# K pages turned on VectorE in 32x32 blocks, and a sample's past split into four partial softmaxes

## The chip, the cores and the metric

The kernel runs on one core of one Trainium2 chip. The metric is the device time of one execution in microseconds (us), lower is better. Three runs of the kernel before gave 971.84, 969.80 and 974.57 us, so the median is 971.84.

## What is computed

One inference step of a two-layer decoder trunk, all in float32, `D_MODEL` 1024, 16 heads of 64. Inputs are a prompt of 512 tokens and 8 sample sequences of 8 new tokens each, whose past of 2048 tokens lies in pages: 16 pages of 128 rows a sample, found through a page table. Layer A is a gated short convolution. Its result gives shared keys, values and log-forget values; layer B is attention over them. The part around the change, cut from the reference:

```python
def _fox_attend(q, fq, qpos, k, v, fk, kpos):
    s = jnp.einsum('nqhd,nkhd->nhqk', q, k).astype(jnp.float32) * (HEAD_DIM ** -0.5)
    s = s + (jnp.transpose(fq, (0, 2, 1))[:, :, :, None]
             - jnp.transpose(fk, (0, 2, 1))[:, :, None, :])
    mask = kpos[None, :] <= qpos[:, None]
    s = jnp.where(mask[None, None], s, -jnp.inf)
    p = jax.nn.softmax(s, axis=-1)
    return jnp.einsum('nqhk,nkhd->nqhd', p.astype(v.dtype), v)

k_past = cache_k[page_table].reshape(nb, -1, N_HEADS, HEAD_DIM)
v_past = cache_v[page_table].reshape(nb, -1, N_HEADS, HEAD_DIM)
```

A sample's attention runs over its 2048 past rows and its 8 new ones; the prompt's over its own 512 rows with a causal mask.

## The kernel before, in words

All is one program of five instruction streams (SP, POOL, ACT, DVE, PE) that wait on semaphores; the order within each is written out by hand. It has four parts: layer A (`mixer`, eight rounds), the output of A in slabs (`out_slab`), eight query blocks (`query`), and then a loop over i = 0..7 (`heads`), followed by a tail that joins the new tokens and makes the output of B.

Round i of the loop does two things at once. It projects K, V and the gate for head pair i, with weights split into a high and a low part (`piece`, L1221; `project(0)`, `(1)`, `(2)`), and does the prompt's attention of that pair in four blocks (`block_scores`, `block_turn`, `block_out`). And it does the past attention of sample i over 32 pages: 16 of K, then 16 of V, each 128 rows by 1024 floats (512 KB).

The pages arrive in a ring of 8 slots in SBUF (`ring`, 4 KB a slot and partition). SP issues all loads of pages, weights, suffix rows and f rows in one order; page n + 8 is loaded when slot n is free (L370 to L377, L431 to L436): for K when the page has been turned (`b_t1`), for V when the product has used it (`b_used`, L434).

In the K stretch, for each page k, PE turns the page in eight 128x128 transposes through two PSUM banks (`turn`, L1201, called under `for k in range(NPG)`); ACT (L666) and DVE (L1009) copy one bank each into `KTS`. After every two pages `unit_scores` (L1404) makes the scores of one unit of 256 rows: the 32 output rows of column group j hold four heads by eight queries, and the query operand `QC` is zero outside of its own heads. DVE adds the forget suffix and takes the maximum (`add_suffix`, L1014). Pieces of `project(0)` and `project(1)` stand between the pages. POOL scales the weights (L501) and copies the next `QC` and `QT`.

Then a bridge: the maximum of the sample, four exponentials on ACT (L707), each of which lets PE turn one group of four 128-column blocks of scores; ACT and DVE copy them to `PTS`. In between stand the turns of the new K and V rows, pieces of `project(2)` and the prompt's block scores.

In the V stretch, for each page k, PE makes four products of 32 by 256 (L1519), accumulated over all 16 pages into bank `OS`:

```python
for j in range(4):
    mm = pe.matmul(PS[32 * j:32 * j + 32, OS, 0:4 * HD], PTS[:, k, 32 * j:32 * j + 32],
                   ring[:, n % RING, 4 * HD * j:4 * HD * (j + 1)],
                   start=(k == 0), stop=(k == NPG - 1), tile_position=(0, 32 * j))
```

Only one quarter of the columns of each 256-wide product belongs to each output row's head. The prompt's steps stand between the pages. At the end ACT copies the result to `OPAST`, and DVE (L1123, L1127) gates and splits the prompt's output of the pair.

In the tail PE makes the new tokens' scores (L1537), DVE and ACT their softmax joined with the past, PE the products (L1565), DVE the merge (L1167, L1169), PE turns it back, while tiles of the output projection (`early_tile`, L1270) fill the gaps.

A float32 matmul leaves two records in the trace, a transpose and a split (float32r) matmul one.

## Time and profile before

| | |
|---|---|
| runs | 971.84, 969.80, 974.57 us |
| profiled execution | 975.04 us, of which the span is 973.2 us |
| granted TensorE clock | 0.996 of full speed |
| loop over the samples | 364 to 899 us |
| instructions in the span | 23705 |
| DMA over the span | 212 GB/s mean; the K and V page loads are 256 of 512 KB |

The page gives each engine's busy share and the span in 40 slices; a view of windows gives the same for any stretch, with the share of time that the 16 DMA engines had packets in flight. TensorE overlaps its matmuls, so the mean of one record is longer than its share of the busy time: costs are taken as busy time divided by count.

### The profile page before, as it was taken

To read this page: it belongs to the slowest core of one execution; us is meant where nothing else is said; L and a number is where in the kernel's file an instruction comes from. 1 tells how busy PE (TensorE), PEld (TensorE's weight loads), DVE (VectorE), ACT (ScalarE), POOL (GpSimd) and SP (SyncE) were. 2 spreads that over 40 slices of the span, in tenths; PEclk is the share of its full clock that TensorE was granted. 3 is DMA by queue.
4 is the path that set the end of the run, shared out by engine and by line. 5 is a ranking of instruction groups with operands and counts; after the bars stand their busy time and mean duration, and the time that the engine had idled before them with its cause. 6 is when DMAs were issued, how large, how long until landed. Compare 5 with 4: busy or idle time off the path is not lost.

```text
span 973.2 us, 23705 instructions
## 1 busy us (share of the span) xinstructions
PE 939.5 (97%) x8516; PEld 802.0 (82%) x8516; DVE 486.6 (50%) x1133; ACT 385.1 (40%) x728; POOL 167.4 (17%) x111
## 2 busy tenths in 40 slices
PE   4999999999999999999999999999999999999998
PEld 4999999999998987868768778688687686776898
DVE  5675444556355334554544544645545545445632
ACT  5333333332144443543444534535434445345210
POOL 2233444332030311102002002011020020000000
PEclk9999999999999999999999999999999999999999
DMA  7233222225343527799799798798996997987412
GB/s 233 66 87 86 86 76 75 85 65 130 120 165 103 174 55 228 254 329 341 237 360 313 249 364 290 247 376 261 315 350 237 362 323 244 365 297 249 142 44 98
DMA packets 133334, 206.41 MB, mean 212 GB/s; under 512 B 8848, under 2 KB 91457, under 8 KB 133171
## 3 DMA queue, kind: packets, MB, share of 16 engines
q1 hardware_dynamic: 121602, 198.35, 60.7%
q10 hardware_dynamic: 11168, 5.51, 2.0%
q0 software_dynamic: 528, 2.10, 0.8%
q8 instruction: 21, 0.34, 0.2%
q14 instruction: 15, 0.11, 0.0%
HBM read 195.29 MB, written 10.63 MB: 212 GB/s over the span
## 4 chain that ended last, share of the span: by engine, by line
PE 82%; DMA 7%; ACT 4%; DVE 4%; issue 2%; SPq 1%; ACTq 0%; DVEq 0%
PE psum L1221 40%; PE psum L1201 16%; PE psum L1270 9%; PE psum L1404 7%; PE psum L1519 4%; DMA page_ring<-in_cache_k 4%; ACT sample_scores L707 2%; DMA w_raw<-in_a_w_out 2%; PE psum L1469 1%; PE psum L1447 1%; DMA residual<-in_x_prompt 1%; PE psum L1319 1%; PE psum L1427 1%; PE psum L1449 1%; DMA page_ring<-in_cache_v 1%
## 5 line engine op out<-in xcount | busy, mean ns | idle before, releaser
L1221 PE MATMUL psum<-xn_high,w_high 128*128 128x256 f32 (+1 forms) x992 | 237.2, 318 | 2.6 <-DVE w_low L832 2.6
L1221 PE MATMUL psum<-xn_low,w_high 128*128 128x256 f32 (+1 forms) x992 | 216.4, 297 | 0.0
L1221 PE MATMUL psum<-xn_high,w_low 128*128 128x256 f32 (+1 forms) x992 | 216.3, 297 | 0.0
L1221 PEld LDWEIGHTS psum<-xn_high,w_high 128*128 128x128 f32 x992 | 163.9, 191 | 20.2 <-issue 16.6
L1221 PEld LDWEIGHTS psum<-xn_high,w_low 128*128 128x128 f32 x992 | 169.0, 191 | 0.0
L1221 PEld LDWEIGHTS psum<-xn_low,w_high 128*128 128x128 f32 x992 | 168.9, 190 | 0.0
L1201 PE MATMUL psum<-constants,page_ring 128*128 128x128 f32 x1024 | 137.5, 277 | 7.7 <-DMA page_ring<-in_cache_k 6.5
L1201 PEld LDWEIGHTS psum<-constants,page_ring 128*128 128x128 f32 x1024 | 114.8, 141 | 35.1 <-issue 33.4
L501 POOL TENSOR_TENSOR w_raw<-w_raw,gains 128x1024 f32<-128x1024 f32 x32 | 60.8, 1899 | 338.9 <-DMA w_raw<-in_b_w_in 220.7
L1009 DVE COPY k_turned_odd<-psum 128x512 f32<-128x512 f32 x64 | 44.2, 691 | 93.5 <-PE psum L1201 93.5
L832 DVE TENSOR_TENSOR w_low<-w_raw,w_high 128x1024 fp32r<-128x1024 f32 x32 | 51.4, 1606 | 72.6 <-ACT w_high L565 72.6
L1009 DVE COPY k_turned<-psum 128x512 f32<-128x512 f32 x64 | 44.2, 690 | 71.5 <-PE psum L1201 71.3
L478 POOL TENSOR_TENSOR w_raw<-w_raw,gains 128x1024 f32<-128x1024 f32 x30 | 62.5, 2083 | 88.7 <-DMA w_raw<-in_a_w_in 88.7
L666 ACT ACTIVATE k_turned<-psum 128x512 f32<-128x512 f32 x64 | 38.2, 597 | 96.5 <-PE psum L1201 96.4
L1519 PE MATMUL psum<-page_ring,p_turned 128*32 128x256 f32 x1024 | 75.2, 388 | 0.9 <-DMA page_ring<-in_cache_v 0.8
L565 ACT ACTIVATE w_high<-w_raw 128x1024 fp32r<-128x1024 f32 x32 | 33.9, 1060 | 89.0 <-PE psum L1221 63.5
L666 ACT ACTIVATE k_turned_odd<-psum 128x512 f32<-128x512 f32 x64 | 38.1, 596 | 71.3 <-PE psum L1201 71.3
L1270 PE MATMUL psum<-w_high,gated_high 128*128 128x256 f32 (+1 forms) x160 | 46.5, 290 | 4.4 <-DVE w_low L859 1.9
L926 DVE TENSOR_TENSOR w_low<-w_raw,w_high 128x1024 fp32r<-128x1024 f32 x30 | 36.9, 1231 | 18.2 <-ACT w_high L615 18.2
L1270 PE MATMUL psum<-w_low,gated_high 128*128 128x256 f32 (+1 forms) x160 | 45.7, 286 | 0.0
L1270 PE MATMUL psum<-w_high,gated_low 128*128 128x256 f32 (+1 forms) x160 | 45.7, 286 | 0.0
L1270 PE MATMUL psum<-w_high_b,gated_high 128*128 128x256 f32 (+1 forms) x160 | 45.3, 283 | 0.1
(236 smaller groups left out, 1420.2 us busy)
## 6 DMA issues: line engine op xcount, KB each, us to landing
page_ring<-in_cache_k SPq DMA_DIRECT2D x128, 512.0 KB, 5.6
page_ring<-in_cache_v SPq DMA_DIRECT2D x128, 512.0 KB, 4.8
w_raw<-in_a_w_in SPq DMA_DIRECT2D x30, 512.0 KB, 4.1
suffix<-suffix_scratch SPq DMA_DIRECT2D x32, 256.0 KB, 4.8
w_raw<-in_b_w_in SPq DMA_DIRECT2D x16, 512.0 KB, 6.2
w_raw<-in_kv_w SPq DMA_DIRECT2D x16, 512.0 KB, 6.1
w_raw<-in_a_w_out SPq DMA_DIRECT2D x4, 1024.0 KB, 5.1
f_broad<-f_scratch SPq DMA_DIRECT2D x8, 512.0 KB, 6.2
```

The source lines that it names most:

```text
L478: pool.tensor_tensor(WR[:, q % 2, :, :], WR[:, q % 2, :, :], gain(G_A), ALU.mult).then_inc(a_scaled, 1)
L501: pool.tensor_tensor(WR[:, slot, :, :], WR[:, slot, :, :], gain(g), ALU.mult).then_inc(b_scaled, 1)
L565: act.activation(WH[:, slot, :, :], WR[:, slot, :, :], ACT.Copy).then_inc(a_high, 1)
L666: return act.activation(out, src, ACT.Copy)
L832: dve.tensor_tensor(WL[:, slot, :, :], WR[:, slot, :, :], WH[:, slot, :, :].bitcast(F32), ALU.subtract).then_inc(a_split, 1)
L926: dve.tensor_tensor(lo, WR[:, slot, :, :], h.bitcast(F32), ALU.subtract).then_inc(b_split, 1)
L1009: return dve.tensor_copy(out, src)
L1201: return pe.transpose(out, src, CT[0:r, C_ID:C_ID + r])
L1221: mm = pe.matmul(PS[:, bank + h, 0:c.stop - c.start], w[:, k, :], x[:, k, c], start=(k == 0 and n == 0), stop=(k == KT - 1 and n == 2))
L1270: mm = pe.matmul(PS[0:r, bank, 0:SLAB], x[:, k, toks(t)], wp[:, k, :], start=(k == 0 and p == 0), stop=(k == KT - 1 and p == 2))
L1404: mm = pe.matmul(PS[32 * j:32 * j + 32, bank, 0:256], QC[:, 2 * j + pp, :], KTS[u % 2][:, 2 * j + pp, :], start=(pp == 0), stop=(pp == 1), ...
L1519: mm = pe.matmul(PS[32 * j:32 * j + 32, OS, 0:4 * HD], PTS[:, k, 32 * j:32 * j + 32], ring[:, n % RING, 4 * HD * j:4 * HD * (j + 1)], star ...
```

## The change

Instead of a whole turn on PE, DVE turns each K page in place in its ring slot, each 32x32 block by itself. After that partition 32a + c of block column m holds, for the rows of quarter a (32 rows), dimension 32m + c. So each quarter of the 128 partitions has its own 32 rows of the page, and 32 of a head's 64 dimensions. The queries are laid out to fit: `QN` holds them with every 32 dimensions repeated on all four quarters, and `QC` is made by POOL for each sample (`spread_queries`), with eight query columns for each quarter and zeros outside of the own one. A score row is now (group of heads j, quarter r, query), its columns (head x in the group, row in the quarter); a head's two halves of dimensions are accumulated (f = 0, 1). Each row's maximum and sum are over one head and a quarter of all past rows: four partial softmaxes for each query, whose maxima (`MS`) and sums (`LS`) have four columns a sample. They are joined once, in the tail.

V goes with it. `vpages` orders a page's rows as (r p): one transfer puts row 32r + p on partition a + 4p, slot r of half a ring; four pages fill every partition of four slots. So V is used by groups of four pages, `b_v` counts whole groups, and SP waits for four V steps before it refills (n = 16 and 20). The turned probabilities (`PTS`) are multiplied by POOL onto the diagonal blocks of a zeroed tile, `PTZ` (one buffer, four times a sample, waiting for the V steps of the group before), so that a product has the rows of its quarter alone.

A K slot is free only when its unit is scored (`b_su`). The scores are 32 matmuls a unit with 64 columns, V 16 a page with 64 columns; all keep 128 rows by 32 columns of weights. The adds of the suffix go by group of four pages and head: four of 128 columns in place of two of 256. The suffix rows are stored in the new order (`SP`). `SS` exponentials are one for each head x over all groups, and PE waits for all four.

Ahead of the loop PE makes `QN` by 16 matmuls of 512 columns with slices of the identity, copied by ACT and DVE; `KTS`, `QZ`, `CK` and `CQ` go. Constants are shorter. In the tail the maxima are turned, joined over the quarters, turned back; the new tokens' scores are 128 matmuls of 8 columns; sums are joined by a matmul with `SUM`; DVE scales `OPAST` by sample (8 multiplies), and 16 matmuls with a summing operand merge the quarters on top of the new tokens' products, so that the result is already turned.

The diff's core (the rest is semaphore counts, placements and the tail):

```diff
@@ -373,10 +396,15 @@
 
         def load_page(b, n):
             page = sp.value_load(PTAB[0:1, bass.ds(b * NPG + n % NPG, 1)], min_val=0, max_val=n_pool - 1)
-            src = (kpages if n < NPG else vpages)[bass.ds(page, 1), :, :]
-            sp.dma_start(ring[:, n % RING, :], src.rearrange("a p n -> (a p) n")).then_inc(b_page[n % RING], 16)
-
-        sp.wait_ge(s_table, 16 * 3)
+            if n < NPG:
+                src = kpages[bass.ds(page, 1), :, :].rearrange("a p n -> (a p) n")
+                sp.dma_start(ring[:, n % RING, :], src).then_inc(b_page[n % RING], 16)
+            else:
+                half, a = n // GROUP % 2, n % GROUP
+                src = vpages[bass.ds(page, 1), :, :, :].rearrange("a p r n -> (a p) r n")
+                sp.dma_start(ring[a:P:GROUP, GROUP * half:GROUP * half + GROUP, :], src).then_inc(b_v[half], 16)
...
                         sp.wait_ge(b_used, NPG * i + n - NPG + 1)
                         sp.dma_start(X[0:rows(t), t, :], h_dram[t * P:t * P + rows(t), :]).then_inc(s_hld, 16)
                 else:
-                    sp.wait_ge(s_table, 16 * 3)
-                    if n < NPG:
-                        sp.wait_ge(b_t1, 24 * i + n + 1)
-                    else:
+                    sp.wait_ge(s_table, 16 * 4)
+                    if n < RING:
+                        sp.wait_ge(b_su, NPG // 2 * i + n // 2 + 1)
+                    elif n < NPG and n % GROUP == 0:
+                        sp.wait_ge(b_su, NPG // 2 * i + (n + GROUP) // 2)
+                    elif NPG <= n < NPG + RING and n % GROUP == 0:
+                        sp.wait_ge(b_used, NPG * i + n - NPG + GROUP)
+                    elif n >= NPG + RING:
                         sp.wait_ge(b_used, NPG * i + n - NPG + 1)
                     load_page(i + (n + RING) // STREAM, (n + RING) % STREAM)
...
+        def spread_queries(b):
+
+            q = QN[:, :, bass.ds(b * NQ, NQ)].unsqueeze(2).to_broadcast([P, 2 * H, GROUP, NQ])
+            own = QM[:, :].unsqueeze(1).unsqueeze(3).to_broadcast([P, 2 * H, GROUP, NQ])
+            pool.tensor_tensor(QC[:, :, :].rearrange("p c (r q) -> p c r q", r=GROUP), q, own, ALU.mult).then_inc(b_qc, 1)
+
...
+        ones = CT[:, T_ONE:T_ONE + 1].unsqueeze(2).unsqueeze(3).to_broadcast([P, GROUP, 4 * XQ, NQ])
 
         def heads(i, last):
...
+            for g in range(NG):
+                pool.wait_ge(b_used, NPG * i + GROUP * g)
+                pool.wait_ge((b_t0f, b_t1f)[g % 2], 8 * i + 3 + g // 2)
+                blocks = PTS[:, GROUP * g:GROUP * g + GROUP, :].rearrange("p x (j r q) -> p r (x j) q", j=XQ, r=GROUP)
+                pool.tensor_tensor(diagonal, blocks, ones, ALU.mult).then_inc(b_pz, 1)
+            if last:
...
-                                     bias=TINY[:, 13:14], accum_out=TINY[:, 16 + c:17 + c])
-                ins.then_inc(b_es, 1)
+            for x in range(XQ):
+                s4 = SS[:, :].rearrange("p (g x n) -> p x g n", g=NG, x=XQ)[:, x]
+                act.activation(s4, s4, ACT.Exp, bias=TB[:, x:x + 1], accum_out=TL[:, x:x + 1]).then_inc(b_es, 1)
...
@@ -1004,52 +1055,48 @@
...
+            def add_suffix(g):
+
+                free, bank = ((b_c0f, C0), (b_c1f, C1))[g % 2]
+                dve.wait_ge(b_sfx[g % 2], (2 * i + g // 2 + 1) * 16)
+                dve.wait_ge(b_su, NPG // 2 * i + 2 * g + 2)
+                dve.memset(TINY[0:1, 32 + g:33 + g], 0.0)
+                for x in range(XQ):
+                    out = SS[:, (XQ * g + x) * P:(XQ * g + x + 1) * P].rearrange("p (n a) -> p a n", a=GROUP)
+                    scored, later = (z.rearrange("p (a x n) -> p x a n", a=GROUP, x=XQ)[:, x]
+                                     for z in (PS[:, bank, :], SFX[:, g % 2, :]))
+                    ins = dve.tensor_tensor_reduce(out, scored, later, 1.0, NEG, ALU.add, ALU.max, TM[:, x, g:g + 1])
+                ins.then_inc(free, 1)
 
             for k in range(NPG):
-                c = (k % 2) * PAGE
-                if k % 2 and k >= 3:
-                    u = k // 2 - 1
-                    if u % 2 == 0:
-                        dve.wait_ge(b_sfx[(u // 2) % 2], (2 * i + u // 4 + 1) * 16)
-                    dve.wait_ge((b_c0, b_c1)[u % 2], 8 * i + u // 2 + 1)
+                dve.wait_ge(b_page[k % RING], (2 * i + k // RING + 1) * 16)
+                dve.transpose(ring[:, k % RING, :], ring[:, k % RING, :]).then_inc(b_kt, 1)
+                if k % GROUP == 1 and k >= GROUP:
+                    add_suffix(k // GROUP - 1)
                 if k == 6:
...
-                turned1(KTS[k // 2 % 2][:, 4:8, c:c + PAGE],
-                        PS[:, T1, :].rearrange("p (k n) -> p k n", k=4)).then_inc(b_t1f, 1)
-                if k % 2 and k >= 3:
-                    add_suffix(k // 2 - 1)
                 if k == 11:
...
@@ -1360,17 +1421,24 @@
         pe.wait_ge(q_rr, KT - 1)
         q_sum()
         pe.wait_ge(s_fnr, 1)
-
+        pe.wait_ge(q_out, KT)
+        pe.wait_ge(s_bf, 6)
+        for c in range(4):
+            for r in range(XQ):
+                mm = pe.matmul(PS[32 * r:32 * r + 32, T0 + c, :].rearrange("p (m n) -> p m n", m=KT),
+                               CT[:, C_ID + 32 * c:C_ID + 32 * c + 32], QF[:, :, SEQ:TOK],
+                               start=True, stop=True, tile_position=(0, 32 * r))
+        mm.then_inc(s_qs, 1)
 
         def heads(i):
             t0, t1 = [0], [0]
...
             def unit_scores(u):
 
-                full, free, bank = ((b_c0, b_c0f, C0), (b_c1, b_c1f, C1))[u % 2]
+                free, bank = ((b_c0f, C0), (b_c1f, C1))[u // 2 % 2]
                 if u == 0:
                     pe.wait_ge(b_qc, i + 1)
-                    pe.wait_ge(q_out, KT)
-                pe.wait_ge(free, 8 * i + u // 2)
-                pe.wait_ge(b_t0f, 24 * i + 2 * u + 2)
-                pe.wait_ge(b_t1f, 24 * i + 2 * u + 2)
-                for pp in range(2):
-                    for j in range(4):
-                        mm = pe.matmul(PS[32 * j:32 * j + 32, bank, 0:256], QC[:, 2 * j + pp, :],
-                                       KTS[u % 2][:, 2 * j + pp, :],
-                                       start=(pp == 0), stop=(pp == 1), tile_position=(0, 32 * j))
-                mm.then_inc(full, 1)
+                    pe.wait_ge(s_qn, 4)
+                if u % 2 == 0:
+                    pe.wait_ge(free, 6 * i + u // 4)
+                pe.wait_ge(b_kt, NPG * i + 2 * u + 2)
+                slot = 2 * u % RING
+                for x in range(XQ):
+                    for f in range(2):
+                        for j in range(QH):
+                            c = 2 * (QH * j + x) + f
+                            out = PS[32 * j:32 * j + 32, bank, 256 * (u % 2):256 * (u % 2) + 256]
+                            mm = pe.matmul(out.rearrange("p (a x n) -> p x a n", a=2, x=XQ)[:, x], QC[:, c, :],
+                                           ring[:, slot:slot + 2, 32 * c:32 * c + 32],
+                                           start=(f == 0), stop=(f == 1), tile_position=(0, 32 * j))
+                mm.then_inc(b_su, 1)
...
-                page = ring[:, k % RING, :]
-                free0()
-                for p in range(4):
-                    mm = turn(PS[:, T0, p * P:(p + 1) * P], page[:, p * P:(p + 1) * P])
-                mm.then_inc(b_t0, 1)
-                free1()
-                for p in range(4):
-                    mm = turn(PS[:, T1, p * P:(p + 1) * P], page[:, (4 + p) * P:(5 + p) * P])
-                mm.then_inc(b_t1, 1)
                 if k == 9:
 
...
             project(2, [3])
 
             for g in range(4):
-                pe.wait_ge(b_es, 4 * i + g + 1)
+                if g == 0:
+                    pe.wait_ge(b_es, 4 * i + 4)
...
-                n = NPG + k
-                pe.wait_ge(b_page[n % RING], (4 * i + n // RING + 1) * 16)
+                g, r = k // GROUP, k % GROUP
                 if k == 0:
                     pe.wait_ge(b_ln, i + 1)
-                if k % 4 == 0:
-                    g = k // 4
-
-                    pe.wait_ge((b_t0f, b_t1f)[g % 2], 24 * i + 19 + g // 2)
-                for j in range(4):
-                    mm = pe.matmul(PS[32 * j:32 * j + 32, OS, 0:4 * HD], PTS[:, k, 32 * j:32 * j + 32],
-                                   ring[:, n % RING, 4 * HD * j:4 * HD * (j + 1)],
-                                   start=(k == 0), stop=(k == NPG - 1), tile_position=(0, 32 * j))
+                    pe.wait_ge(b_sot, i)
+                if r == 0:
+                    pe.wait_ge(b_v[g % 2], 16 * GROUP * (2 * i + g // 2 + 1))
+                    pe.wait_ge(b_pz, NG * i + g + 1)
+                for x in range(XQ):
+                    for j in range(QH):
+                        h = QH * j + x
+                        c = 4 * P * r + P * x + 32 * j
+                        mm = pe.matmul(PS[32 * j:32 * j + 32, OS, x * HD:(x + 1) * HD], PTZ[:, c:c + 32],
+                                       ring[:, GROUP * (g % 2) + r, h * HD:(h + 1) * HD],
+                                       start=(k == 0 and x == 0), stop=(k == NPG - 1 and x == XQ - 1),
+                                       skip_group_check=True, tile_position=(0, 32 * j))
                 mm.then_inc(b_used, 1)
-            assert t0[0] == t1[0] == 24
+            assert t0[0] == t1[0] == 8
 
         with pe.Fori(0, NB) as i:
             heads(i)
 
 
```

The tail's merge (added lines):

```diff
+        pe.wait_ge(m_pd, XQ)
+        for m in range(KT):
+            for e in range(2):
+                h = 2 * m + e
+                pe.matmul(PS[64 * e:64 * e + 64, C0, m * NS:(m + 1) * NS], VS[:, h * HD:(h + 1) * HD],
+                          PD[:, h, :, :].rearrange("p b q -> p (b q)"),
+                          start=(m == 0), stop=False, skip_group_check=True, tile_position=(0, 64 * e))
+        pe.wait_ge(m_w, NB)
+        first = SUM[:, :].rearrange("p (j r q) -> p j r q", j=XQ, r=GROUP)[:, :, 0, :]
+        merged = PS[:, C0, :].rearrange("p (j y b q) -> p y b j q", j=XQ, y=2, b=NB)
         for b in range(NB):
...
-                mm.then_inc(m_pv, 1)
-        for n in (3, 4, 5):
+            for y in range(2):
```

## Rows read from the trace of the kernel before

**Rows 1.** The page, busy us (share of the span) and instructions.
```profile
PE 939.5 (97%) x8516; PEld 802.0 (82%) x8516; DVE 486.6 (50%) x1133; ACT 385.1 (40%) x728; POOL 167.4 (17%) x111
```

**Rows 2.** Windows, one sample: us, busy by engine (records), clock, DMA share, GB/s.
```profile
633.60:700.30 66.70, 65.42 (x655) 49.58 (x655) 33.40 (x97) 30.55 (x66) 8.14 (x6) 1.00 0.92 309
```

**Rows 3.** Timeline, the loop's first and last TensorE pieces: start us, us, what.
```profile
364.09 1.04 PE L1201 MATMUL psum<-constants,page_ring 128*128 128x128 f32 x8
...
898.16 0.64 PE L1519 MATMUL psum<-page_ring,p_turned 128*32 128x256 f32 x8 [0.18 <-DMA page_ring<-in_cache_v]
```

**Rows 4.** Windows, stretches of sample 566 to 633.6 us, same columns.
```profile
566.00:606.00 40.00, 39.92 (x367) 33.47 (x368) 16.05 (x37) 14.34 (x25) 7.54 (x5) 0.96 0.92 317
606.00:614.20 8.20, 8.13 (x67) 6.90 (x65) 5.20 (x16) 5.09 (x12) 0.00 (x0) 1.00 0.55 202
614.20:633.60 19.40, 18.63 (x225) 10.65 (x223) 11.79 (x43) 10.38 (x27) 0.62 (x1) 1.00 0.90 289
```

**Rows 5.** Groups by line and shape, TensorE: busy us, mean ns | idle.
```profile
L1201 PE MATMUL psum<-constants,page_ring 128*128 128x128 f32 x1024 | 137.5, 277 | 7.7 <-DMA page_ring<-in_cache_k 6.5 <-DVE k_turned L1009 1.2
L1519 PE MATMUL psum<-page_ring,p_turned 128*32 128x256 f32 x1024 | 75.2, 388 | 0.9 <-DMA page_ring<-in_cache_v 0.8
...
L1404 PE MATMUL psum<-k_turned_odd,q_current 128*32 128x256 f32 x512 | 34.3, 385 | 0.8 <-DVE k_turned_odd L1009 0.2
...
L1537 PE MATMUL psum<-ks_t,q_spread 128*32 128x64 f32 x128 | 2.0, 220 | 0.2 <-issue 0.2
```

**Rows 6.** Groups by line and shape, VectorE, whole run.
```profile
L832 DVE TENSOR_TENSOR w_low<-w_raw,w_high 128x1024 fp32r<-128x1024 f32 x32 | 51.4, 1606 | 72.6 <-ACT w_high L565 72.6
...
L1009 DVE COPY k_turned<-psum 128x512 f32<-128x512 f32 x64 | 44.2, 690 | 71.5 <-PE psum L1201 71.3 <-DVE f_query L997 0.2
L926 DVE TENSOR_TENSOR w_low<-w_raw,w_high 128x1024 fp32r<-128x1024 f32 x30 | 36.9, 1231 | 18.2 <-ACT w_high L615 18.2
```

**Rows 7.** Groups by line and shape, VectorE, 633.6 to 700.3 us.
```profile
L1087 DVE TENSOR_SCALAR probs<-probs,tiny 128x512 f32<-128x512 f32 x2 | 0.9, 484 | 0.0
...
L1073 DVE CUSTOM_DVE_ANT_0 probs_odd<-psum,f_broad 128x128 f32<-128x128 f32 x2 | 0.5, 288 | 0.0
```

**Rows 8.** Timeline, where one sample ends and the next begins.
```profile
632.26 0.64 PE L1519 MATMUL psum<-page_ring,p_turned 128*32 128x256 f32 x8
...
634.53 0.69 DVE L1127 TENSOR_TENSOR gated_low<-squares,gated_high 128x512 f32 x1 [0.93 <-ACT gated_high L766]
```

**Rows 9.** Groups by line and shape, POOL.
```profile
L501 POOL TENSOR_TENSOR w_raw<-w_raw,gains 128x1024 f32<-128x1024 f32 x32 | 60.8, 1899 | 338.9 <-DMA w_raw<-in_b_w_in 220.7 <-DMA w_raw<-in_kv_w 118.2
```

**Rows 10.** Timeline, the first exponential of a sample's scores.
```profile
608.68 0.71 ACT L707 ACTIVATE sample_scores<-sample_scores,tiny 128x512 f32<-128x512 f32 x1
```

**Rows 11.** Timeline, last V product of groups 0, 1 and 2 of four.
```profile
618.94 0.64 PE L1519 MATMUL psum<-page_ring,p_turned 128*32 128x256 f32 x8
...
624.62 0.64 PE L1519 MATMUL psum<-page_ring,p_turned 128*32 128x256 f32 x8
...
628.22 1.07 PE L1519 MATMUL psum<-page_ring,p_turned 128*32 128x256 f32 x16
```

**Rows 12.** Timeline of SP's queue, four V pages issued.
```profile
601.67 4.10 SPq L377 DMA_DIRECT2D page_ring<-in_cache_v  x4
```

**Rows 13.** DMA queues (packets, MB, share), issues (us to landing), 432 to 830 us.
```profile
q1 hardware_dynamic: 51189, 118.58, 86.5%
q10 hardware_dynamic: 6816, 3.34, 3.0%
...
page_ring<-in_cache_v SPq DMA_DIRECT2D x96, 512.0 KB, 4.7
page_ring<-in_cache_k SPq DMA_DIRECT2D x94, 512.0 KB, 5.8
```

**Rows 14.** DMA queues in the first sample, 364 to 432 us.
```profile
q8 instruction: 6, 0.10, 0.6%
```

**Rows 15.** Timeline, the last query is written.
```profile
366.61 0.57 DVE L978 SCALAR_TENSOR_TENSOR q_spread<-psum,gain_q,rsqrt 64x64 f32<-64x64 f32 x2
```

426 lines of the change are left out of this document (231 added, 195 removed).

## The prediction

> **What bounds the kernel now.** I read the page first: TensorE is busy for 939.5 of 973.2 us [rows 1]. Then one sample: from 633.6 to 700.3 us TensorE worked 65.4 of 66.7 us, VectorE 33.4, ScalarE 30.6, and the DMA share was 0.92 [rows 2]. So two resources are near their ends, and taking work from TensorE helps only until the pages' transfers pace the sample. The loop over the samples runs from 364.1 to 898.8 us [rows 3], eight times 66.8. Three stretches cut one sample [rows 4]: K pages (40 us, TensorE busy throughout, VectorE 16.0), a bridge of 8.2 us, the V stretch (19.4 us). In the V stretch the share is 0.90 and in the bridge only 0.55: the ring is full and waits for the first V step.
>
> **The turns.** 1024 K turns are 137.5 us [rows 5], 134 ns each, 17.2 us a sample. TensorE's K stretch falls from 40 to about 23 us, the sample's TensorE work from 66 to 49.
>
> **Scores and V products.** A product of 256 columns becomes four of 64, 32 output rows each; the columns stay the same. A record of 256 columns takes 67 ns in the scores (34.3 us by 512) and 73 in V; the one row with 64 columns and the same 128x32 weights has 128 records in 2.0 us, 15.6 ns each, a quarter [rows 5]. So I take no change. There are 1024 such records a sample in place of 256. Bounds: below, nothing gained, since the columns stay; above, half as much again for each in a long stream (second rival).
> Ahead of all rows stands a rule: the Trainium skill, "TensorE: Matmul & The Clock Gate", section "Wait — 56ns, not 53.3ns?", says that matmuls never start closer than about 25 ns however few columns they have. The 15.6 ns of [rows 5] are against it, in a burst of 128 records; no row shows 1024 a sample.
>
> **VectorE.** Removed in the K stretch: 16 copies of 0.69 us [rows 6] and eight suffix adds of 256 columns. Added: 16 block turns of 128x1024 in SBUF. No row has one. Nearest is the subtraction of L926, 128x1024, 1.23 us [rows 6]. Below: a TENSOR_SCALAR of 512 at 0.48 us [rows 7] makes 0.8 us for 1024. Above: 1.61 us, the same subtraction in the mixers (L832, [rows 6]). I take 1.23. The suffix adds become 4 of 128 columns for each group of four pages; a 128-column one is 0.29 us [rows 7], with hand-over 0.34, so 1.4 us a group. I count from E, the end of the last V product of the sample before (632.9, [rows 8]). VectorE then still has its last subtraction (L1127, to 635.2 or E+2.3, [rows 8]); then 16 turns (19.7), three groups (4.1), one low_b (1.2) and, estimated from the same rows by columns, KN_T and KS (1.2): last page turned at E+28.5, last scores at E+29.5. TensorE could be there at E+23: **VectorE paces the K stretch**, 29.5 us in place of 40. ScalarE loses 16 copies and is on no path. POOL adds a query spread of 1024 elements (1.9 us by its row of that size, [rows 9]) after the last scores, needed 25 us later.
>
> **Bridge.** The chain behind the last scores is four adds (1.4), the shifts (0.5), and now all four exponentials before the first turn of scores (4 x 0.71, [rows 10]; before, the first was enough), a turn (0.5), a copy (0.6), and the new POOL product of 512 elements (half of 1.9, say 1.1), with hand-overs about 8 us. TensorE's own work in the bridge is 8.1 us [rows 4], most of it ahead of these turns. I take 9 us, against 8.2.
>
> **V stretch.** The groups of four V steps took 5.3, 5.7, 4.1 and 3.6 us (from 614.2 to the ends at 619.5, 625.2, 629.3, 632.9, [rows 4, 8, 11]). V now comes in whole groups, since each transfer writes all four slots on every fourth partition. SP used to refill after each V step; now it waits for four, and K pages of the next sample are queued behind that wait. SP issues four pages in 4.1 us [rows 12] and a V page lands 4.7 us after its issue [rows 13], so a group lands 3.1 + 4.7 = 7.8 us after its first issue. Group 2, asked for at 5.3+0.1, lands at 13.2; TensorE arrives at 11.0 and **waits 2.2 us**. Group 3, asked for at 11.1, lands at 18.9; TensorE arrives at 17.3 and waits 1.6. The POOL product between groups (1.1) lies beside a project and block scores, longer than it (groups 1, 2), and beside transfers (group 3). The stretch is 18.7 + 3.8 = 22.5 us. That each V transfer writes 32 partitions costs nothing by my sum: size and row length (4 KB) are as before. Bounds: nothing, and a doubled transfer, the fourth rival.
> **DMA.** A sample moves its 20 MB in 0.9 x 66.8 = 60 us of busy share, part of it packets in flight beside others: 118.58 MB took 86.5% of 398 us [rows 13], while the first V pages came at 1.03 us by their issue [rows 12]. I estimate 32 pages at 1.3 us, and some 13 us for weights, suffixes, f rows and stores: 55 us. With the K-page requests spread over 29 us this keeps up. K page 0 is asked for after V step 9 as before and is there by E.
> A sample is 29.5 + 9 + 22.5 = **61 us** against 66.8: 8 x 5.8 = 46 us gained.
>
> **Instruction stream.** A sample has 655 TensorE records and as many weight loads [rows 2]. In its first pass 6 instruction packets of 16 KB come in (0.10 MB, [rows 14]), in the passes from 432 to 830 us none: only q1 and q10 stand there [rows 13]. The body was kept. It becomes 655 - 128 + 768 = 1295 of each, some 190 KB. No row says whether that is kept. If not, each of 7 jumps back waits for a transfer: between nothing and the 5.8 us of a loaded K page [rows 13]. I take the middle, 2.9. TensorE has some 1.5 us to spare ahead of the second score unit, on which VectorE waits in order; 1.3 us count, **9 us** in all.
> The Trainium skill, "Runtime: NRT & Kernel Launch", section "Instruction fetch mechanics", gives TensorE's store as 128 KiB and says that a taken branch to a page no longer held stalls; the trace agrees as far as the old body goes. By that page the new body is not kept.
>
> **Ahead and behind.** The first sample started at 364.1, under the last query. Now the quartered queries need all queries (written by 367.2, [rows 15]): 32 records of 512 columns (4.2 us at twice 67 ns), copies (1.4), spreading (1.9) beside the first project. Start at 371.3: **+7 us**. The suffix and mask edits move the same elements: 0. In the tail 64 records of 256 columns and 16 + 8 turns go; 256 tiny records, 32 with full weights (134 ns each) and a chain between VectorE and TensorE come, behind eight multiplies of some 0.4: **+2 us**, between -3 and +8.
>
> **Sum.** -46 + 9 + 7 + 2 = -28 us. The profiled execution took 975.0 us (span 973.2), 3.2 above the median of 971.84. From the median: **943 us**.
>
> **Rivals.**
> 1. *Cheap block turns.* At 0.8 us VectorE needs 7 us less, TensorE (23 and its hand-overs) paces the K stretch and a sample is some 57 us: 943 - 32 = 911; with the body kept 902. For it: the 512 columns in SBUF (0.48) beside those from PSUM (0.69), [rows 6, 7]. Against: a turn is no plain copy. 0.18.
> 2. *Small records cost more in a long stream.* At half as much again, 23.4 ns, 1024 cost 8 us more: 4 in the scores (TensorE at 29 with its hand-overs, beside VectorE's 29.5: some 0.7 late) and 1.0 a V group, of which 3 us stay behind the waits. A sample is 64.7 us: 943 + 8 x 3.7 = 973. For it: one burst is all that speaks against. Against: the 15.6 ns is in proportion to the columns. 0.15 (0.04 faster, 0.06 same, 0.05 slower). By the 25 ns of the Trainium skill's "TensorE: Matmul & The Clock Gate" the same sum gives an estimate of 980.
> 3. *Slower, by VectorE.* Each 0.1 us on a block turn makes a sample 1.6 us longer, as the K stretch waits for 16 in turn: from 1.45 us on the gain is gone. At 1.61 us: 943 + 8 x 6.1 = 992. At two passes (2.3 us) 1080. For it: VectorE has no such operation here and the mixers' row is above that point. Against: L926, the row of this loop, is at 1.2. 0.12.
> 4. *The spread V transfer is slow.* If 16 V pages took double, DMA would need 55 + 21 = 76 us a sample: 1060. Only in favour: no row has the pattern. 0.04.
> 5. *The stall between samples or the groups' wait is worse*, 3 to 4 us each sample: about 970. 0.04, same. That the change fails to remove the turns can't be.
> My forecast has 0.47.
>
> **Numbers.** Faster by over 0.5% (what a measurement here can tell, 4.9 us): 0.47 + 0.18 + 0.04 = 0.69. Same: 0.06 + 0.04 = 0.10. Slower: 0.05 + 0.12 + 0.04 = 0.21. The range leaves out the ends of rivals 1, 3 and 4: 905 to 984. The forecast's own range is 925 to 962.
>
> **What would show it.** Right: a sample near 61 us; the block turn at 1.2 us; TensorE idle in the K stretch waiting for VectorE, and before the third and fourth V group for the V transfer; 64-column records at 16 ns each; instruction packets in every sample. Wrong: turns far from 1.2 us, records above 20 ns, TensorE waiting on K pages (then DMA paces), or a V page landing after more than 6 us.

## The result, and the profile after

The changed kernel takes **1080.3 us** (median of 4 runs, 1079.52 to 1082.57) beside 970.82 us for the kernel before on the same chip: a ratio of 1.114, 95% interval 1.108 to 1.120, so 11% slower where 3% faster was forecast. The profiled execution took 1082.57 us, its span 1080.8. Ratios and intervals leave out an execution clearly slower than the others of its kernel, which touches two runs below: one of 1032.22 us in experiment 1 and one of 1011.44 in experiment 3.

The page of the changed kernel first: busy time by engine, the granted clock by slices (in tenths), the packets of instructions.

```profile
PE 912.4 (84%) x13780; PEld 824.3 (76%) x13780; DVE 570.8 (53%) x1268; ACT 308.6 (29%) x586; POOL 219.1 (20%) x151
PEclk9999999999999999698698799898798797796789
q8 instruction: 111, 1.82, 0.8%
```

TensorE is busy for less time than before (912 against 939 us, [rows 1]) in a span that is 108 us longer. Its clock, full nearly everywhere before, dips once or twice in every sample from the second on. Instruction packets went from 21 to 111. VectorE is at 53%: no engine is full any more.

The last product with the gate of each sample (L1170, L1123 before) comes at 443.1 us in the first sample and at 997.9 in the last: 79.3 us a sample, where it was 66.7 ((898.0 - 431.4) / 7). Of the 107.6 us of longer span, 88 are those seven periods, 12 lie up to the end of the first sample, 8 behind the last. One sample in three windows, K stretch, bridge and V stretch (columns: us, busy time of TensorE, weight loads, VectorE, ScalarE, GpSimd, then granted clock, DMA share, GB/s):

```profile
601.50:638.40 36.90, 29.18 (x650) 26.05 (x650) 24.78 (x49) 5.80 (x11) 6.16 (x3) 0.81 0.73 235
638.40:651.50 13.10, 8.92 (x70) 7.59 (x70) 7.24 (x26) 5.60 (x13) 4.75 (x3) 1.00 1.02 318
651.50:681.10 29.60, 22.15 (x606) 17.71 (x606) 12.12 (x42) 9.64 (x26) 3.67 (x4) 0.88 0.76 257
```

Predicted were 29.5, 9 and 22.5 us; each came out 4 to 7 us longer. In the first and the last window the clock is 0.81 and 0.88, TensorE is busy for 29.18 of 36.90 and 22.15 of 29.60 us, and the DMA share is about 0.75: neither TensorE nor the transfers are full there. What TensorE waited for, in the whole run (columns: us in total, times, longest):

```profile
PE psum L1282 <- issue: 44.0, 14, 5.6
PE psum L1584 <- issue: 30.7, 21, 2.3
PE psum L1584 <- DMA page_ring<-in_cache_v: 25.0, 14, 3.7
PE psum L1282 <- ACT squares L738: 15.1, 8, 2.1
PE psum L1584 <- POOL p_spread L574: 5.7, 6, 1.8
PE psum L1476 <- DVE page_ring L1077: 5.1, 7, 2.0
```

The greatest item, 75 us of "issue" ahead of projections (L1282) and V products (L1584), is time in which TensorE waited for nothing that the profile shows. The wait for VectorE's turns, which was to pace the K stretch, is only 5.1 us. A wait that the sum had at nothing is the fourth line, 1.9 us a sample: projections stand behind a squaring on ScalarE (L738), which waits for VectorE to read the same bank (L1085), and VectorE does that in order, behind seven turns and the first suffix adds. Where the 44 us stand is seen at the jump from one sample to the next, TensorE first and VectorE behind it (start, duration, operation, in brackets the idle time before it):

```profile
601.41 0.65 PE L1584 MATMUL psum<-page_ring,p_spread 128*32 128x64 f32 x32
607.62 0.82 PE L1282 MATMUL psum<-xn_high,w_high 128*128 128x256 f32 x2 [5.56 <-issue]
608.24 0.68 PE L1282 MATMUL psum<-xn_low,w_high 128*128 128x256 f32 x2
608.72 0.68 PE L1282 MATMUL psum<-xn_high,w_low 128*128 128x256 f32 x2
...
612.94 0.43 PE L1282 MATMUL psum<-xn_high,w_low 128*128 128x256 f32 x2
613.20 0.43 PE L1282 MATMUL psum<-xn_high,w_high 128*128 128x256 f32 x2
```

```profile
603.89 6.87 DVE L1077 STREAM_TRANSPOSE page_ring<-page_ring 128x1024 f32<-128x1024 f32 x6
618.11 0.38 DVE L1072 CUSTOM_DVE_ANT_1 sample_scores<-psum,suffix 128x128 f32<-128x128 f32 x1 [7.34 <-issue]
```

The last V product ends at 602.1, the first projection starts at 607.6. For the next 5 us the pairs start 0.48 us apart, from 613 on 0.27: the granted clock is 0.51 from 607.7 to 612.9 us and 1.00 from 613 to 618.9, so after the idle time TensorE runs at the lower of its two levels. The seven idle times like this one are 4.5 to 5.6 us long. So the first scores are late, and VectorE, which has turned six pages by 610.8, stands idle for 7.3 us in front of the suffix add of the first group, with ten more turns in order behind it. The queue of instruction packets in the seven later samples, 443 to 997 us (packets, MB, share):

```profile
q8 instruction: 84, 1.38, 1.1%
```

That is 12 packets of 16 KB a sample, where the kernel before fetched none after its first pass [rows 13, 14].

The operations that the prediction priced without a row (columns: count, busy us, mean ns, then idle time):

```profile
L1077 DVE STREAM_TRANSPOSE page_ring<-page_ring 128x1024 f32<-128x1024 f32 x128 | 150.3, 1217 | 1.0 <-DMA page_ring<-in_cache_k 1.0
L1476 PE MATMUL psum<-page_ring,q_current 128*32 128x64 f32 x4096 | 77.0, 230 | 7.6 <-DVE page_ring L1077 5.1 <-issue 2.4
```

The block turn took 1.22 us (1.23 was taken). At the full clock a unit of scores is 64 records in 1.03 us, 16.1 ns each, and a V step 32 records in 0.57 us, 17.9 ns; no change of the cost by column, 16.8 and 18.3 ns, was taken. Over the whole run, with the stretches at the lower clock, they are 18.8 ns (77.0 us by 4096) and 25.5 ns (L1584, 104.5 us by 4096).

The bridge: GpSimd's queue in front of the first V product.

```profile
646.72 1.90 POOL L537 TENSOR_TENSOR w_raw<-w_raw,gains 128x1024 f32<-128x1024 f32 x1 [13.95 <-DMA w_raw<-in_kv_w]
648.58 1.90 POOL L548 TENSOR_TENSOR q_current<-q_quarters,own_quarter 128x1024 f32<-128x1024 f32 x1
650.43 1.04 POOL L574 TENSOR_TENSOR p_spread<-p_turned,constants 128x512 f32<-128x512 f32 x1
```

A weight scaling, waiting for its transfer, and the query spread for the next sample are ahead of the product that TensorE needs. Then the V stretch: the third group, and gaps of the stream inside it.

```profile
662.01 0.89 PE L1584 MATMUL psum<-page_ring,p_spread 128*32 128x64 f32 x32
668.00 1.94 PE L1584 MATMUL psum<-page_ring,p_spread 128*32 128x64 f32 x64 [3.66 <-DMA page_ring<-in_cache_v]
670.90 0.63 PE L1584 MATMUL psum<-page_ring,p_spread 128*32 128x64 f32 x26
673.29 0.76 PE L1584 MATMUL psum<-page_ring,p_spread 128*32 128x64 f32 x38 [1.76 <-issue]
675.33 1.08 PE L1584 MATMUL psum<-page_ring,p_spread 128*32 128x64 f32 x32 [0.43 <-POOL p_spread L574]
```

```profile
657.77 10.64 SPq L405 DMA_DIRECT2D page_ring<-in_cache_v  x8
```

The third group is asked for at 657.8 and its products start at 668.0; two V steps then take 1.94 us in place of 1.1, at a granted clock of 0.50. The gap ahead of 673.3 splits a V step behind its 26th record, where no wait stands in the code.

Last, the tail: from the end of the loop's last sample to the end, 8 us more than before. Its largest new piece:

```profile
1022.99 7.03 PE L1653 MATMUL psum<-sum_quarters,o_past 128*128 128x32 f32 x32
```

The granted clock is 0.50 through these records.

### The profile page after: what moved, and what is told of

Same layout as the page of the kernel before. It is cut to its first block, busy times and chain, and to the rows that moved or that the text cites. A ratio compares the mean times of both kernels' runs of the same rounds, so it can differ in the third digit from the quotient of the medians.

```text
span 1080.8 us, 33756 instructions
## 1 busy us (share of the span) xinstructions
PE 912.4 (84%) x13780; PEld 824.3 (76%) x13780; DVE 570.8 (53%) x1268; ACT 308.6 (29%) x586; POOL 219.1 (20%) x151
## 4 chain that ended last, share of the span: by engine, by line
PE 57%; issue 18%; DVE 11%; DMA 6%; ACT 3%; SPq 3%; POOL 1%; DVEq 0%; ACTq 0%; POOLq 0%
PE psum L1282 31%; PE psum L1331 8%; PE psum L1584 6%; DVE page_ring L1077 5%; PE psum L1262 4%; DMA page_ring<-in_cache_v 4%; PE psum L1476 3%; SPq L405 1%; SPq L398 1%; ACT sample_scores L762 1%; PE psum L1531 1%; DMA page_ring<-in_cache_k 1%; DMA w_raw<-in_a_w_out 1%; PE psum L1509 1%; DVE sample_scores L1072 1%
## 5 line engine op out<-in xcount | busy, mean ns | idle before, releaser
L1282 PE MATMUL psum<-xn_high,w_high 128*128 128x256 f32 (+1 forms) x992 | 242.0, 324 | 62.2 <-issue 44.0
L1282 PEld LDWEIGHTS psum<-xn_high,w_high 128*128 128x128 f32 x992 | 173.3, 200 | 79.7 <-issue 54.3
L1282 PE MATMUL psum<-xn_low,w_high 128*128 128x256 f32 (+1 forms) x992 | 224.2, 306 | 0.0
L1282 PE MATMUL psum<-xn_high,w_low 128*128 128x256 f32 (+1 forms) x992 | 223.8, 306 | 0.0
L1282 PEld LDWEIGHTS psum<-xn_high,w_low 128*128 128x128 f32 x992 | 176.9, 199 | 0.0
L1282 PEld LDWEIGHTS psum<-xn_low,w_high 128*128 128x128 f32 x992 | 176.8, 199 | 0.0
L1584 PE MATMUL psum<-page_ring,p_spread 128*32 128x64 f32 x4096 | 104.5, 256 | 61.4 <-issue 30.7
L1077 DVE STREAM_TRANSPOSE page_ring<-page_ring 128x1024 f32<-128x1024 f32 x128 | 150.3, 1217 | 1.0 <-DMA page_ring<-in_cache_k 1.0
L1584 PEld LDWEIGHTS psum<-page_ring,p_spread 128*32 128x32 f32 x4096 | 82.4, 131 | 86.9 <-issue 73.6
L1476 PE MATMUL psum<-page_ring,q_current 128*32 128x64 f32 x4096 | 77.0, 230 | 7.6 <-DVE page_ring L1077 5.1
L1476 PEld LDWEIGHTS psum<-page_ring,q_current 128*32 128x32 f32 x4096 | 65.2, 116 | 20.5 <-issue 12.7
L1060 DVE COPY probs_t<-psum 128x512 f32<-128x512 f32 (+3 forms) x32 | 15.7, 491 | 112.7 <-PE psum L1262 112.7
L574 POOL TENSOR_TENSOR p_spread<-p_turned,constants 128x512 f32<-128x512 f32 x32 | 33.4, 1044 | 182.8 <-PE psum L1584 166.2
L1072 DVE CUSTOM_DVE_ANT_1 sample_scores<-psum,suffix 128x128 f32<-128x128 f32 x128 | 35.0, 384 | 58.9 <-issue 58.9
L981 DVE TENSOR_TENSOR w_low<-w_raw,w_high 128x1024 fp32r<-128x1024 f32 x30 | 42.8, 1425 | 25.5 <-ACT w_high L676 25.5
L976 DVE TENSOR_TENSOR residual<-psum,residual 128x256 f32<-128x256 f32 (+1 forms) x40 | 16.7, 421 | 72.2 <-PE psum L1331 72.1
```

The lines of the kernel that those rows point to most:

```text
L981: dve.tensor_tensor(lo, WR[:, slot, :, :], h.bitcast(F32), ALU.subtract).then_inc(b_split, 1)
L1072: ins = dve.tensor_tensor_reduce(out, scored, later, 1.0, NEG, ALU.add, ALU.max, TM[:, x, g:g + 1])
L1077: dve.transpose(ring[:, k % RING, :], ring[:, k % RING, :]).then_inc(b_kt, 1)
L1282: mm = pe.matmul(PS[:, bank + h, 0:c.stop - c.start], w[:, k, :], x[:, k, c], start=(k == 0 and n == 0), stop=(k == KT - 1 and n == 2))
L1476: mm = pe.matmul(out.rearrange("p (a x n) -> p x a n", a=2, x=XQ)[:, x], QC[:, c, :], ring[:, slot:slot + 2, 32 * c:32 * c + 32], start=(f ...
L1584: mm = pe.matmul(PS[32 * j:32 * j + 32, OS, x * HD:(x + 1) * HD], PTZ[:, c:c + 32], ring[:, GROUP * (g % 2) + r, h * HD:(h + 1) * HD], sta ...
```

## Experiments

The theory after the result (A): TensorE's loop body, the instructions of one sample with some 1294 records, is no longer kept from one pass to the next, so each jump back to its start stalls TensorE for 5.5 to 7 us, and slow clock and a late VectorE follow. Rivals: TensorE would have to wait there anyway (B), every packet stalls (C), small records are dear (D).

**1. Jump removed.** In the changed kernel, and as a control in the one before, TensorE's eight samples are written out one behind the other:

```diff
-        with pe.Fori(0, NB) as i:
-            heads(i)
+        for i in range(NB):
+            heads(i)
```

> The kernel after, with TensorE's eight samples written out one behind the other, so that TensorE never jumps back. Theory A (the loop body of 1295 TensorE records a sample is too large to be kept, each jump back stalls TensorE for 5.5 to 7 us, the stall lowers the granted clock for some 5 us and makes VectorE's first suffix add late): the 5 to 7 us of idle time ahead of each sample's first record go, a sample falls from 79.3 to 68 to 71 us, the total from 1080 to 990 to 1015. Instruction packets stay near 100. Rival B (TensorE would have to wait there anyway, for VectorE's turns, the page transfers or the small records' issue): the idle time moves to another releaser and the total stays above 1055. Rival C (it isn't the jump but every instruction packet that stalls TensorE): the idle time is spread over the sample as stalls of 1 to 2 us and the total stays within 20 us of 1080.

Measured: 1025.65 us (1016.15 to 1032.22), ratio to before 1.053 [1.046, 1.060]; a sample takes 71.0 us ((934.0 - 437.2) / 7), 8.3 less. B and C as stated are out: the idle time at the jump is gone, and only a part came back as waits for V and GpSimd. It is A, though the total lies above its 990 to 1015. The gaps ahead of V products fell too, from 30.7 to 4.9 us, so most of them came with the loop; those ahead of scores rose from 2.4 to 10.3. What TensorE now waited for:

```profile
PE psum L1584 <- DMA page_ring<-in_cache_v: 38.8, 16, 4.1
PE psum L1584 <- POOL p_spread L574: 13.2, 6, 3.2
PE psum L1476 <- issue: 10.3, 9, 2.7
PE psum L1584 <- issue: 4.9, 5, 2.3
```

The three stretches of one sample, without the jump (columns as above):

```profile
652.90:682.70 29.80, 26.19 (x621) 23.37 (x620) 25.08 (x48) 5.81 (x11) 5.17 (x3) 0.94 0.89 302
682.70:694.80 12.10, 8.89 (x72) 7.55 (x73) 8.38 (x30) 6.69 (x16) 4.75 (x3) 1.00 0.97 326
694.80:724.70 29.90, 23.34 (x607) 18.75 (x607) 11.35 (x38) 8.55 (x23) 3.81 (x4) 0.80 0.76 266
```

Over the last seven samples the K stretch takes 29.6 to 31.6 us, the bridge 10.1 to 13.4, the V stretch 27.0 to 29.9. So the K stretch is at its forecast of 29.5 once the jump is gone, and the V stretch is not.

> The kernel before, with TensorE's eight samples written out. Its loop body fetches nothing after the first pass, so this prices straight fetching by itself: about 45 more instruction packets. Theory A: hidden, within 5 us of the kernel before (971). Rival C (every packet stalls TensorE by 1 to 2 us): 40 to 80 us more, near 1030.

Measured: 974.44 us, ratio 1.0042 [1.0022, 1.0062], a sample 66.6 us, 36 packets in seven samples. 36 x 16 KB / (7 x 655) is 128 bytes for a record and its weight load. Straight fetching of the old body costs 0.4%.

**2. The body alone made larger.** The kernel before, with V products cut (here all 16 steps):

```diff
-                for j in range(4):
-                    mm = pe.matmul(PS[32 * j:32 * j + 32, OS, 0:4 * HD], PTS[:, k, 32 * j:32 * j + 32],
-                                   ring[:, n % RING, 4 * HD * j:4 * HD * (j + 1)],
+                for x in range(4):
+                    for j in range(4):
+                        c = 4 * HD * j + HD * x
+                        mm = pe.matmul(PS[32 * j:32 * j + 32, OS, HD * x:HD * x + HD], PTS[:, k, 32 * j:32 * j + 32],
+                                       ring[:, n % RING, c:c + HD],
...
```

> The kernel before, with each V product of 256 columns cut into four of 64: the results and columns are the same, TensorE's loop body grows from 655 to 847 records. Theory A: no more instruction packets than before, if the body is still kept, and the total within 6 us of 971; if it isn't kept any more, 6 to 9 packets a sample and 5 to 6 us a jump, near 1015. Rival D (64-column records cost more than a quarter of 256-column ones): each V stretch grows by 192 x the extra, 1.5 us a sample at 24 ns a record, so about 985 with no instruction packets.

> As the run with cut V products, and the score products of 256 columns cut into four of 64 too: 1039 TensorE records a sample. VectorE, ScalarE, GpSimd and all transfers of pages are as in the kernel before. Theory A: the body is refetched in every sample, 8 to 11 instruction packets of 16 KB each pass, TensorE stands idle 5 to 7 us ahead of each sample's first record and the granted clock falls behind it: 1020 to 1040. Rival B (the stall needs the change's VectorE order or V transfers): within 10 us of 971. Rival D: 985 to 1000 with the time spread over the products and no idle time at the jump.

Measured: 1079.83 us (ratio 1.115 [1.111, 1.119]) and 1082.59 us (1.116 [1.112, 1.120]), samples of 80.6 and 81.2 us. Both expectations had the bodies too small: the trace shows each fp32 product as two records, so they are 1039 and 1423. With VectorE, GpSimd and the V layout of the kernel before, 384 more TensorE records a sample cost 110 us, as much as the whole change; 384 further ones, 3 us more. With V products cut the span is 103 us longer: 43 us of idle time at the seven jumps (5.3 to 6.8 us each), 32 of other gaps for instructions, most of them ahead of V products (21.9), and 35 of longer busy time (974.5 us for 939.5), less 7 us of waits for pages. The jump of the kernel with cut V products:

```profile
599.42 0.76 PE L1521 MATMUL psum<-page_ring,p_turned 128*32 128x64 f32 x32
605.45 1.97 PE L1201 MATMUL psum<-constants,page_ring 128*128 128x128 f32 x8 [5.26 <-issue]
607.07 0.83 PE L1221 MATMUL psum<-xn_high,w_high 128*128 128x256 f32 x2
...
611.52 0.42 PE L1221 MATMUL psum<-xn_high,w_low 128*128 128x256 f32 x2 [1.71 <-issue]
```

It is like the changed kernel's jump: more than 5 us idle, then half pace; here a second gap follows. Rival B needs the change's VectorE order and falls here too.

**3. Where does the body stop being kept?** Only the first V steps cut (`cut = 4 if k < 8 else 1`, with 8, 14 and 4):

> First a correction of the counts in the two runs before: the trace shows each fp32 product of a page as two records, so V products cut in four make TensorE's body 1039 records and not 847, and the scores cut too make it 1423. Here only the first 8 of the 16 V steps are cut into 64 columns: 655 + 192 = 847 records, 108 KB at the 128 bytes a record pair that the fetched packets show. Theory A (the body is kept up to about 128 KB, and all or nothing beyond): no more instruction packets than in the kernel before (about 21), no idle time at the jump, 965 to 977. Rival E (what is kept is less, or the cost grows with every record added): 7 or more packets a sample and 1010 to 1080.

> The first 14 of 16 V steps cut: 655 + 336 = 991 records, 127 KB, against 1039 records (133 KB) in the run with all 16 cut, which was 110 us slower. Theory A: still kept, 965 to 978: two V steps more or less would then carry over 100 us. Rival E: above 1060.

Measured: 1033.1 us (ratio 1.065 [1.063, 1.067]) and 1058.77 us (1.092 [1.090, 1.095]). Theory A's 128 KB missed both: 847 records are refetched in every sample (63 packets in seven), with 4.4 to 6.3 us of idle time at each jump. There is no cliff of 100 us between 991 and 1039 records. Behind the jump's stall the cost goes on rising with gaps in the V stretch (22.4 us in all at 991 records, none of note at 847). The last 48 records cost 21 us, of which 17 are longer stalls at the jumps (25.2 us in all at 991, 42.6 at 1039); why the stalls are shorter at 991 isn't shown.

> The kernel before with the first 4 V steps cut into 64 columns: 655 + 96 = 751 TensorE records, 96 KB. The uncut one (655, 84 KB) fetches nothing after its first pass, the one with 8 steps cut (847, 108 KB) fetches 7 to 8 packets a sample and stalls 3 to 6 us at each jump. Theory A' (body and what is fetched ahead past the jump must fit in 128 KB together; three or four packets were ahead at 847 records): kept or refetched in part, 968 to 1000. Theory E (what is kept ends just above 84 KB): 1015 to 1030.

Measured: 999.91 us (992.09 to 1011.44; ratio 1.026 [1.020, 1.032]). The profiled execution is the one of 1011.44. Some jumps stall in it and some don't; the pieces of over 5 us that the chain puts down to "issue":

```profile
431.94 5.82 issue
506.83 5.25 issue
713.57 5.31 issue
788.12 5.44 issue
933.38 5.20 issue
```

Four stand at jumps, the fifth at the exit from the loop, 124 records into the tail. Packets show the same: 9 in each of the four samples that stall (432 to 507, 507 to 581, 713.5 to 788, 788 to 862 us), none in the other three. A period with a stall is 74.9 us (431.94 to 506.83), one without 66.4 (the first page turns of two samples, at 581.14 and 647.52): **a jump to a body that is gone costs 8 us**, of which TensorE stands idle for 5.7 to 6.4; the rest is the half clock behind it and, at three of the four, a second gap of 0.8 to 1.4 us. The change in state comes between 84 KB (always kept) and 108 KB (never). The four executions differ by up to 19 us, the price of two such jumps; the other three have no trace.

**4. Is it the stream itself, too?** Both products cut, and written out:

> The kernel before with score and V products cut into 64 columns (1423 TensorE records a sample) and TensorE's eight samples written out: the looped one took 1082.59, the uncut written-out one 974.44. Theory A (of its 112 us nearly all is the refetch behind the jump; small records cost their quarter): 975 to 985. Theory I (64-column records use up instructions faster than they come: 32 records of 128 bytes each in 0.57 us, so even without a jump the stream stalls at packet ends inside runs of small products): 985 to 1010, with 2 to 4 us a sample of idle time inside the V stretch. Rival D (small records themselves cost more): 985 to 1000 without idle time.

Measured: 1019.67 us (ratio 1.050 [1.046, 1.054]), a sample 73.0 us against 66.6 uncut and 81.2 looped. Theory I is right and stronger than it said:

```profile
PE psum L1522 <- issue: 25.6, 13, 3.2
PE psum L1470 <- issue: 4.5, 1, 4.5
PE psum L1201 <- issue: 4.4, 2, 4.0
PE psum L1405 <- issue: 2.1, 3, 1.3
```

37 us of gaps, nearly all in or just behind runs of small products: 128 records of 128 bytes are one packet, and TensorE uses them up in an estimated 2.3 us (four V steps of 0.57). The V row also grew by 11 us, to 21.0 ns a record where a quarter of 73 is 18.3 (busy 85.9 us by 4096; 75.2 by 1024 before, [rows 5]). Rival D has at most that: a V step at the full clock takes 0.58 us here, 18 ns a record, so part of the 11 us is the lower clock behind the gaps.

**5. GpSimd's order.** In the changed kernel, the second weight scaling goes behind the second spreading of probabilities, the query spread behind the fourth:

```diff
-            if not last:
-                scale_b(1, 7 + 2 * i, G_KV)
-                pool.wait_ge(b_su, NPG // 2 * (i + 1))
-                spread_queries(i + 1)
             for g in range(NG):
...
                 pool.tensor_tensor(diagonal, blocks, ones, ALU.mult).then_inc(b_pz, 1)
+                if g == 1 and not last:
+                    scale_b(1, 7 + 2 * i, G_KV)
+            if not last:
+                pool.wait_ge(b_su, NPG // 2 * (i + 1))
+                spread_queries(i + 1)
```

> The kernel after, with GpSimd's order changed alone: the second scaling of weights goes behind the second spreading of probabilities, and the spreading of the next sample's queries behind the fourth, so that the first spreading of probabilities no longer waits behind 3.8 us of other work. Theory F (GpSimd's queue lies on the bridge's chain): the bridge falls from 13 to 10 or 11 us, 2 to 3 us a sample, total 1056 to 1066. Rival G (the V transfers and the jump's stall set the end anyway, and what is gained in the bridge is waited for at the third V group or at the next sample's first score): within 8 us of 1080.

> GpSimd's order changed and TensorE's samples written out, both. Without the stall at the jump the gain of the GpSimd order should be whole: 2 to 3 us a sample below the written-out run's 1025.65, 1000 to 1010 (theory F). Rival G: within 8 us of 1025. Either way it stays above the kernel before (970), since a K stretch paced by VectorE (31 us), a bridge of 9 and a V stretch of 29 make 69 us against 66.7.

Measured: 1059.05 us (1054.48 to 1063.38), 21 less, 2.5 us a sample ((976.2 - 439.0) / 7 is 76.7): theory F. The bridge takes 10.2 to 12.6 us where it took 11.1 to 14.1. Written out it is 1014.07 us (1012.09 to 1014.78), 12 less and not 16 to 25, with a bridge of 10.1 to 10.6 us: with the jump gone, part of the gain comes back as gaps for instructions ahead of V products (12.7 us, from 4.9) and as waits for V (40.5 us, from 38.8).

**6. V groups free their slots earlier.** On top of experiment 5, the same TensorE instructions, V steps 0 to 3 back to back, then 4 to 7 nearly so (`part(n)` is the piece `project(2, [n])`, which stood at steps 1, 2 and 4):

```diff
-            steps = {0: [(block_scores, 1)], 3: [(block_turn, 0)], 4: [(block_scores, 2)], 5: [(block_out, 0)],
-                     7: [(block_turn, 1)], 8: [(block_scores, 3), (block_out, 1)], 10: [(block_turn, 2)],
-                     12: [(block_out, 2)], 13: [(block_turn, 3)], 15: [(block_out, 3)]}
+            steps = {0: [(block_scores, 1), (part, 5)], 4: [(part, 6), (block_turn, 0), (block_scores, 2)],
+                     5: [(part, 7)], 8: [(block_out, 0), (block_turn, 1), (block_scores, 3), (block_out, 1),
+                                         (block_turn, 2)],
+                     12: [(block_out, 2), (block_turn, 3)], 15: [(block_out, 3)]}
```

> On top of the run with GpSimd's order changed and TensorE written out (1014.07): TensorE's order in the V stretch alone. The four V steps of the first group go back to back, ahead of a project piece, a block turn and block scores that stood between them, and the second group's likewise as far as the block chain allows; that work comes later, where TensorE stood waiting for V. The same instructions. Theory H (the V stretch is paced by when the first two groups free their slots, since only whole groups can be refilled and their 4 MB then take some 17 us to land): group 0 ends 3 to 4 us earlier, the V stretch falls from 27 to 29 us to 22 to 24, total 965 to 990. Rival G (TensorE's work and the order of the block chain set the stretch): within 10 us of 1014.

> The same order of V steps with TensorE's loop kept (base 1059.05). Theory A with H: the stalls of the jump and inside the V stretch stay (5 to 6 us and 2 to 4 us a sample), so 1015 to 1035, 40 to 50 above the written-out run of this call. If the refetching were hidden behind the V waits it would be within 15 us of it.

Measured: written out 998.3 us (993.76 to 1008.45), looped 1039.75 us (1033.9 to 1047.36), so 16 and 19 less than without (13 and 17 by the ratios to the kernel before on each chip). A sample of the written-out one is 67.1 us ((905.8 - 436.3) / 7). Theory H has the direction, and falls short of its 965 to 990. The V stretch went to 23.7 to 27.8 us where 22 to 24 were expected, and the waits of V products changed their kind:

```profile
PE psum L1587 <- issue: 24.9, 14, 3.4
PE psum L1587 <- DMA page_ring<-in_cache_v: 19.9, 10, 4.2
PE psum L1477 <- issue: 15.2, 10, 2.9
```

V steps back to back use up instructions fastest, and the gaps for instructions (12.7 us at these products without the reordering) took more than half of what the V waits (40.5 us) gave back.

> On top of the run with GpSimd's order changed and TensorE written out (1014.07): the V pages of the third and fourth group (8 of 16 a sample) are not loaded, and their products use what lies in the ring. It prices all waits for late V pages and the transfers' load: theory H: 5 to 7 us a sample, 958 to 975 in all. Rival G: above 995.

Measured, one execution: 960.0 us, and a sample of 62.7 us ((871.9 - 432.9) / 7). This run leaves out the loads of 8 of the 16 V pages and only gives a price. Against 69.7 us of its base ((924.0 - 436.3) / 7), the late V groups, with all that their transfers do to the rest, cost 7 us a sample.

## Why the prediction was wrong

The miss is 137 us (1080.3 for 943), and two steps of about the same size make most of it. Writing TensorE's samples out takes 55 us away, of which 9 were forecast: 46. What is left is a sample of 71.0 us for 61, some 80 us in eight: 6 us a sample in the V stretch (28.7 on average for 22.5), 3 in the bridge (12.0 for 9), 1 in the K stretch (30.4 for 29.5). The tail adds 5.

**The first step that failed** is the one called "Instruction stream". It had the size of the body right (1295 records), named the refetch, and bounded a stall at 5.8 us; but it then put 1.3 us of 2.9 on the path, 9 us in all. Measured: a stall of 4.5 to 5.6 us at each jump, within that bound, and 8.3 us a sample by removing the jump alone, 55 us in all (experiment 1); 5.3 to 7.0 us at the jumps of the kernels with cut products (experiment 2). Three things were missing. The stall was taken at half its bound without a row that spoke for half. The slack was looked for in the second score unit; next to none showed, since the half clock behind the stall makes that unit later still, and VectorE, in order, stood 7.3 us in front of its suffix add with ten turns behind it. And the packets were counted only at the jump: within runs of small products they are late as well, in the loop (30.7 us ahead of V products) and without a jump (4.6 us of gaps a sample in experiment 4).

**The second step that failed** is the V stretch. Its cause was right, and the waits for V, 25.0 us by 8, are 3.1 us a sample where 3.8 stood; written out, where no stall at the jump hides a part, they are 4.9 (38.8 by 8). Mis-sized was what hangs on them: the landing of a group (9.1 to 10.2 us from its first issue, not 7.8, since four issues took 5.3 us and not 4.1, with a DMA queue that then holds eight pages), and V steps at half clock behind each wait (two in 1.94 us in place of 1.1). Without the late groups a sample is 62.7 us. That isn't the 61 forecast met: the forecast without its 3.8 us of waits is 57.2, and some 4 of the 5.5 us between are gaps for instructions (26 us in seven samples).

**The bridge** was 13.1 us and not 9. The sum had the new GpSimd product and the query spread, but put the spread "needed 25 us later" and off the path; both it and a weight scaling stand ahead of the product in the same queue. Reordering gave 12 to 21 us and left a bridge of 10.1 to 10.6 us, written out.

**Ahead and behind.** The first sample's projections start at 371.2 us (371.3 forecast). That the two agree is luck: the last query was written at 365.8 and not 367.2, and the 32 records took 5.3 us (L1428, 365.9 to 371.3, clock 0.59) and not 4.2. The tail is 7.5 us longer, not 2: the 32 merging records took 218 ns each (7.0 us by 32) and not 134, all at a clock of 0.50, which the sum didn't have; and a gap of 2.4 us falls into the 256 tiny records.

**What held.** The block turn (1.22 us), the query spread (1.89) and the probability spread (1.04), the small records at the full clock (16.1 and 17.9 ns), a V page with 32 partitions landing in 5.3 us: rivals 1, 3 and 4 are out by these rows. VectorE does pace the K stretch, at 29.6 to 31.6 us for 29.5, when TensorE's samples are written out. Rival 3 names 1080 us, the time measured; that is chance, since it stands there for a turn of 2.3 us. Rival 5 was the mechanism, in both its parts, and had 0.04; for the jump it was too small, 3 to 4 us a sample where 7 came on top of the 1.3 counted, and it should have been priced with the refetch as certain. Rival 2 was right for another reason: long streams of small records are dearer, by the instructions they use up and the lower clock behind the gaps (18.8 and 25.5 ns on average, above the 20 ns named as a sign of being wrong) more than by their own 16 to 18 ns. The first sample, which has no jump ahead of it, took 71.9 us (371.2 to 443.1) and would have told against 61 by itself.

On the two rules quoted. The row of 128 records spoke against the 25 ns of the Trainium skill's "TensorE: Matmul & The Clock Gate", section "Wait — 56ns, not 53.3ns?", and 4096 records of scores now do, in units at 16.1 ns each and 18.8 on average with the lower clock in them. The rule of the Trainium skill's "Runtime: NRT & Kernel Launch", section "Instruction fetch mechanics", that a taken branch to a page no longer held stalls, agrees with every loop body of 108 KB and more here; its 128 KiB do not describe when, since 108 KB were refetched at every jump and 96 KB at four of seven. Its statement that crossing into the next block of instructions is mostly hidden fits the old body written out (974 against 970 us) and not runs of small products.

Does any version beat both kernels? None that computes everything. The best, written out with both orders changed, takes 998.3 us, 3% over the kernel before. In its profiled execution (993.76 us) the sample is at the old 66.7 us to within 0.4; of the 19 us more of span, 11 are in the tail, 5 up to the end of the first sample and 3 between.
